# Out projection and down products of the samples' 64 tokens: two products instead of three

## The chip, the cores and the metric

The kernel runs on one core of a Trainium2 chip. The metric is the device time of one execution in microseconds (us), and the number compared is the median of several. Engines are named as in the profile: PE (TensorE, with PEld for its weight loads), DVE (VectorE), ACT (ScalarE), POOL (GpSimd) and SP (SyncE, which here only issues DMAs).

## The reference, cut to what matters

One layer of a hybrid decoder (sparse attention beside a gated delta rule) runs over 1024 prompt tokens and over 64 sample tokens (8 sequences of 8) with the same weights. The change touches its last part, which works on a token axis of 1088 rows:

```
mix = concat([o_a, o_b])              # 1088 x 1024, attention heads and delta rule heads
x   = x + mix @ w_out                 # out projection, 1024 x 1024
hm  = rmsnorm(x, norm_mlp)
x   = x + square(relu(hm @ w_up)) @ w_down     # up 1024 x 4096, down 4096 x 1024
y   = rmsnorm(x, norm_final)
```

All of it is float32.

## The kernel before

**Splitting.** TensorE multiplies in a rounded float32 form (fp32r). To keep precision, each operand is split: ScalarE rounds it (`hi`), and VectorE subtracts that from the original (`lo`). `split_product` (lines 2533 to 2535) then issues three products into one PSUM bank: hi x hi, hi x lo of the weights, lo of the activations x hi. The fourth, lo x lo, is left out.

**Sizes.** P is 128, D is 1024, KD = 8 is D in blocks of 128, TOK is 1088 tokens, SEQ is 1024, NS is 64. Tokens come in NT + 1 = 9 row blocks: t = 0 to 7 are 128 prompt tokens each, and t = 8 (t == NT) is the samples' 64. `rows_of(t)` gives 128 or 64. Output columns come in two halves (i = 0, 1) of 512, one PSUM bank each.

**Out projection** (`stage_output_projection`). Three groups g of three row blocks, six banks each (bank j holds row block 3g + j // 2, half j % 2). In each group the loop runs over the 8 blocks f of the contraction and over the six banks, three products each, with the activations as the stationary operand and 512 columns of the weights moving. The rounded weights come through a ring of three blocks: DMA on SP, cast on ACT (L2631), subtraction on DVE (L2668). The activations `mix` are rounded into `h_hi` (L2634) and `h_lo` (L2672). When a group's banks are complete, DVE adds all six to `x2` (L2710), and then, in the next group's loop, each row block is squared and rooted on ACT (L2641, L2643), scaled on DVE (L2677, L2681), transposed on PE (L2600), multiplied by the gain on DVE (L2692), and split again for the MLP (L2662 on ACT, L2696 on DVE). For the third group, which holds row blocks 6, 7 and 8, there is no next group, and this work stands alone at the end of the stage. DVE adds all six banks there before it scales row block 6.

**MLP** (`stage_mlp`). 32 blocks of 128 hidden columns. An "up" step makes one of them for all tokens (three pieces of 364, 364 and 360 tokens in banks 0 to 3, with the weights stationary). A "down" step takes two of them (e = 2f and 2f + 1) and runs over the nine row blocks and both halves: six products in one of the banks 4 to 7, in rotation, which DVE then adds to `x2` (L2908). The order is written out by hand in `steps`: up 0, up 1, then for each of 16 down steps "up 2g + 2, down g, up 2g + 3". PE waits for bank n of a down step until addition n - 4 is done. Behind a down step's additions DVE makes the low parts of the next two blocks of down weights (L2873, after ACT's cast L2830), and then the squares of the next up step (L2918, after ACT's relu L2847). The hidden activations are split by ACT (L2852) and DVE (L2888) into `hid_hi` and `hid_lo`. In the last down step (step 15) DVE also does the final norm: behind row block t's additions comes `final(t - 1)` (L2880, L2882), which waits for ACT's squares and root of that row block (L2860, L2863), and at the end `final(7)` and `final(8)`.

The samples' row block t = 8 is the last of each down step and of the third group. Its products are 64 columns of the stationary wide and leave the upper 64 partitions of their bank unused.

## Time and profile before

| | |
|---|---|
| median of the runs | 2143.38 us (3 runs, 2138.87 to 2144.5) |
| profiled execution | 2143.51 us |
| its span, first to last instruction | 2141.7 us |
| mean granted TensorE clock | 0.945 |
| PE busy | 1924.3 us, 90% of the span |
| DVE busy | 1178.0 us, 55% |
| ACT busy | 682.3 us, 32% |
| POOL busy | 251.6 us, 12% |

The out projection runs from about 1222 to 1346 us of the span (its first cast to its last DVE operation), and the MLP from there to the end. Matmuls are pipelined, so the recorded length of one is longer than the distance from its start to the next one's start. Where products follow each other, it is that distance that counts.

### The profile page before, as it was taken

To read this page: it belongs to the slowest core of one execution; us is meant where nothing else is said; L and a number is where in the kernel's file an instruction comes from. 1 tells how busy PE (TensorE), PEld (TensorE's weight loads), DVE (VectorE), ACT (ScalarE), POOL (GpSimd) and SP (SyncE) were. 2 spreads that over 40 slices of the span, in tenths; PEclk is the share of its full clock that TensorE was granted. 3 is DMA by queue.
4 is the path that set the end of the run, shared out by engine and by line. 5 is a ranking of instruction groups with operands and counts; after the bars stand their busy time and mean duration, and the time that the engine had idled before them with its cause. 6 is when DMAs were issued, how large, how long until landed. Compare 5 with 4: busy or idle time off the path is not lost. (4 is left out here: it accounts for less than half of the span.)

```text
span 2141.7 us, 33279 instructions
## 1 busy us (share of the span) xinstructions
PE 1924.3 (90%) x12648; PEld 1601.5 (75%) x12648; DVE 1178.0 (55%) x2298; ACT 682.3 (32%) x1373; POOL 251.6 (12%) x294
## 2 busy tenths in 40 slices
PE   5999999883589986898999699799999999999998
PEld 5888899883278874566544287788888999998886
DVE  3275588999556646764333266344444444444446
ACT  5332257652423322553322144321111212221113
POOL 4324332210211000001133100000000000000000
PEclk8999999996699996999999799899999999999999
DMA  5324322110110004404898452211111111111102
GB/s 147 80 66 128 87 80 60 30 40 0 51 41 2 2 2 158 143 1 140 291 325 299 145 197 65 69 62 48 40 40 40 40 40 50 40 42 67 40 30 84
DMA packets 121931, 177.33 MB, mean 83 GB/s; under 512 B 33208, under 2 KB 73785, under 8 KB 121644
## 3 DMA queue, kind: packets, MB, share of 16 engines
q1 hardware_dynamic: 104428, 118.05, 17.0%
q0 software_dynamic: 17344, 57.16, 8.5%
q8 instruction: 100, 1.64, 0.3%
q14 instruction: 59, 0.48, 0.1%
HBM read 156.64 MB, written 18.01 MB: 82 GB/s over the span
## 5 line engine op out<-in xcount | busy, mean ns | idle before, releaser
L2533 PE MATMUL banks<-front_h_hi,front_w_hi 128*128 128x364 f32 (+2 forms) x744 | 257.7, 346 | 23.8 <-POOL front_w_lo L627 9.9
L2533 PE MATMUL banks<-h_hi,ml_up_hi 128*128 128x364 f32 (+1 forms) x768 | 253.2, 330 | 10.1 <-DVE ml_up_lo L2869 10.1
L2534 PE MATMUL banks<-h_lo,ml_up_hi 128*128 128x364 f32 (+1 forms) x768 | 253.1, 329 | 0.0
L2535 PE MATMUL banks<-h_hi,ml_up_lo 128*128 128x364 f32 (+1 forms) x768 | 253.0, 329 | 0.0
L2534 PE MATMUL banks<-front_h_lo,front_w_hi 128*128 128x364 f32 (+2 forms) x744 | 250.0, 336 | 0.0
L2535 PE MATMUL banks<-front_h_hi,front_w_lo 128*128 128x364 f32 (+2 forms) x744 | 250.0, 336 | 0.0
L2908 DVE TENSOR_TENSOR x<-x,banks 128x512 f32<-128x512 f32 x256 | 175.8, 687 | 125.5 <-PE banks L2535 125.3
L2533 PE MATMUL banks<-ml_down_hi,ml_hid_hi 128*128 128x512 f32 (+1 forms) x576 | 224.5, 390 | 2.5 <-DVE ml_hid_lo L2888 2.5
L2534 PE MATMUL banks<-ml_down_lo,ml_hid_hi 128*128 128x512 f32 (+1 forms) x576 | 224.4, 390 | 0.0
L2535 PE MATMUL banks<-ml_down_hi,ml_hid_lo 128*128 128x512 f32 (+1 forms) x576 | 224.1, 389 | 0.0
L296 DVE TENSOR_SCALAR_CACHE_REDUCE work<-arena,work 128x384 bf16<-128x384 f32 (+5 forms) x194 | 176.1, 958 | 1.0 <-issue 0.3
L2533 PEld LDWEIGHTS banks<-front_h_hi,front_w_hi 128*128 128x128 f32 (+1 forms) x744 | 143.5, 193 | 41.5 <-POOL front_w_lo L627 11.8
L2918 DVE TENSOR_TENSOR arena<-arena 128x364 f32<-128x364 f32 (+1 forms) x96 | 51.6, 537 | 209.7 <-ACT arena L2847 209.7
L2533 PEld LDWEIGHTS banks<-h_hi,ml_up_hi 128*128 128x128 f32 x768 | 145.0, 189 | 11.7 <-DVE ml_up_lo L2869 10.3
L2534 PEld LDWEIGHTS banks<-h_lo,ml_up_hi 128*128 128x128 f32 x768 | 145.1, 189 | 0.7
L2535 PEld LDWEIGHTS banks<-h_hi,ml_up_lo 128*128 128x128 f32 x768 | 145.0, 189 | 0.0
L2534 PEld LDWEIGHTS banks<-front_h_lo,front_w_hi 128*128 128x128 f32 (+1 forms) x744 | 143.6, 193 | 0.8
L2535 PEld LDWEIGHTS banks<-front_h_hi,front_w_lo 128*128 128x128 f32 (+1 forms) x744 | 143.0, 192 | 0.9
L2830 ACT CAST ml_down_hi<-arena 128x1024 fp32r<-128x1024 f32 x32 | 32.1, 1048 | 293.9 <-PE banks L2535 293.5
L2533 PEld LDWEIGHTS banks<-ml_down_hi,ml_hid_hi 128*128 128x128 f32 (+1 forms) x576 | 104.7, 182 | 27.4 <-DVE ml_hid_lo L2888 2.8
L2535 PEld LDWEIGHTS banks<-ml_down_hi,ml_hid_lo 128*128 128x128 f32 (+1 forms) x576 | 104.7, 182 | 26.2
L2534 PEld LDWEIGHTS banks<-ml_down_lo,ml_hid_hi 128*128 128x128 f32 (+1 forms) x576 | 104.7, 182 | 25.3
(432 smaller groups left out, 3276.1 us busy)
## 6 DMA issues: line engine op xcount, KB each, us to landing
upper<-in_cache_k SPq DMA_DIRECT2D x128, 256.0 KB, 3.9
upper<-in_cache_v POOLq DMA_DIRECT2D x112, 256.0 KB, 4.3
arena<-in_w_up SPq DMA_DIRECT2D x32, 512.0 KB, 4.1
arena<-in_w_down SPq DMA_DIRECT2D x32, 512.0 KB, 5.5
work<-in_w_in POOLq DMA_DIRECT2D x30, 512.0 KB, 4.6
op_raw<-in_w_out SPq DMA_DIRECT2D x24, 512.0 KB, 3.7
arena<-in_x_prompt SPq DMA_DIRECT2D x8, 512.0 KB, 5.9
upper<-in_cache_v SPq DMA_DIRECT2D x16, 256.0 KB, 3.8
```

Of the source, the lines that this page charges most:

```text
L296: dve.tensor_scalar(junk, sc[0:rows, :], than, 0.0, op, ALU.add, accum_out=out[0:rows, i:i + 1]).then_inc(self.counted, 1)
L2533: pe.matmul(out, lh, rh, start=start, stop=False)
L2534: pe.matmul(out, lh, rl, start=False, stop=False)
L2535: return pe.matmul(out, ll, rh, start=False, stop=stop)
L2830: act.copy(dhi[:, n % 2, :], raw_down[:, n % 2, :]).then_inc(down_hi, 1)
L2908: dve.tensor_tensor(part, part, k.psum[4 + n % 4][0:r, :], ALU.add).then_inc(added, 1)
L2918: dve.tensor_tensor(tmp[:, j, 0:w], tmp[:, j, 0:w], tmp[:, j, 0:w], ALU.mult).then_inc(squared, 1)
```

## The change

For the samples' row block the high and the low part of the activations now lie side by side: `h_hi` gets 64 more columns (1088 to 1151), and the low part of the samples' 64 columns is written there instead of into `h_lo`; `hid_hi` likewise, while `hid_lo` loses its 64. One product with these 128 columns as the stationary gives hi x hi in the bank's partitions 0 to 63 and lo x hi in 64 to 127. A second product, with the 64 high columns, adds hi x (weights' lo) to partitions 0 to 63. That makes two products instead of three (`split_product_samples`). DVE then adds the upper half of the bank to `x2` and, after a wait for that (semaphore `low_added`), the lower half: two additions in place of one.

Each subtraction that makes a low part and covers the samples' columns becomes two instructions, since they go to different tensors.

```diff
--- before.py
+++ after.py
@@ -226,7 +226,7 @@
         x2 = enter(nc.sbuf_tensor("x2", [P, NT, D], F32))
         self.x2 = [x2[:, t, :] for t in range(NT)] + [self.view(self.hT_at, D)]
         self.x2_prompt = x2
-        self.h_hi = enter(nc.sbuf_tensor("h_hi", [P, KD, TOK], F32R))
+        self.h_hi = enter(nc.sbuf_tensor("h_hi", [P, KD, TOK + NS], F32R))
         self.h_lo = enter(nc.sbuf_tensor("h_lo", [P, KD, TOK], F32R))
 
     def sem(self, name):
@@ -2535,6 +2535,17 @@
     return pe.matmul(out, ll, rh, start=False, stop=stop)
 
 
+def split_product_samples(pe, bank, both, right, start, stop):
+
+
+    rh, rl = right
+    if start:
+        pe.matmul(bank, both, rh, start=True, stop=False)
+        return pe.matmul(bank[0:NS, :], both[:, 0:NS], rl, start=False, stop=False)
+    pe.matmul(bank[0:NS, :], both[:, 0:NS], rl, start=False, stop=False)
+    return pe.matmul(bank, both, rh, start=False, stop=stop)
+
+
 def stage_output_projection(k):
 
 
@@ -2560,6 +2571,7 @@
              "squared", "rooted", "rstd", "normed", "turned", "kept", "rounded", "rest")
     (mix_hi, mix_lo, w_hi, w_lo, made, used, added,
      squared, rooted, scaled, normed, turned, kept, rounded, rest) = (k.sem("op_" + n) for n in names)
+    low_added = k.low_added = k.sem("low_added")
     xp = a["x_prompt"][0].rearrange("(t p) d -> p t d", p=P)
     xs = a["x_sample"].rearrange("b t d -> (b t) d")
     wv = a["w_out"][0].rearrange("(k p) n -> p k n", p=P)
@@ -2614,7 +2626,10 @@
                             cols = slice(t * P, t * P + rows_of(t))
                             left = k.h_hi[:, f, cols], k.h_lo[:, f, cols]
                             right = whi[:, (g * KD + f) % RING, i * 512:(i + 1) * 512], wlo[:, (g * KD + f) % RING, i * 512:(i + 1) * 512]
-                            last = split_product(pe, k.psum[j][0:rows_of(t), :], left, right, f == 0, f == KD - 1)
+                            if t < NT:
+                                last = split_product(pe, k.psum[j], left, right, f == 0, f == KD - 1)
+                            else:
+                                last = split_product_samples(pe, k.psum[j], k.h_hi[:, f, SEQ:TOK + NS], right, f == 0, f == KD - 1)
                             if f == KD - 1:
                                 last.then_inc(made, 1)
                         if f < KD - 1:
@@ -2631,7 +2646,7 @@
                 act.copy(whi[:, n % RING, :], raw[:, n % RING, :]).then_inc(w_hi, 1)
 
             def round_mix(f):
-                act.copy(k.h_hi[:, f, :], mix[:, f, :]).then_inc(mix_hi, 1)
+                act.copy(k.h_hi[:, f, 0:TOK], mix[:, f, :]).then_inc(mix_hi, 1)
 
             def length(t):
                 r = rows_of(t)
@@ -2669,7 +2684,8 @@
 
             def rest_of_mix(f):
                 dve.wait_ge(mix_hi, f + 1)
-                dve.tensor_tensor(k.h_lo[:, f, :], mix[:, f, :], k.h_hi[:, f, :], ALU.subtract).then_inc(mix_lo, 1)
+                dve.tensor_tensor(k.h_hi[:, f, TOK:], mix[:, f, SEQ:], k.h_hi[:, f, SEQ:TOK], ALU.subtract)
+                dve.tensor_tensor(k.h_lo[:, f, 0:SEQ], mix[:, f, 0:SEQ], k.h_hi[:, f, 0:SEQ], ALU.subtract).then_inc(mix_lo, 1)
 
             def scale(t):
                 r = rows_of(t)
@@ -2707,6 +2723,9 @@
                         r = rows_of(t)
                         part = k.x2[t][0:r, i * 512:(i + 1) * 512]
                         dve.wait_ge(made, NP * (g - 1) + j + 1)
+                        if t == NT:
+                            dve.tensor_tensor(part, part, k.psum[j][NS:P, :], ALU.add).then_inc(low_added, 1)
+                            dve.wait_ge(low_added, i + 1)
                         dve.tensor_tensor(part, part, k.psum[j][0:r, :], ALU.add).then_inc(added, 1)
                     n = g * KD + f + RING - 1
                     if n < KD:
@@ -2730,6 +2749,7 @@
     up_sem, down_sem = k.sems("ml_up_landed", 2), k.sems("ml_down_landed", 2)
     names = ("up_rounded", "up_rest", "down_rounded", "down_rest", "up", "relu", "square", "hid_rounded", "hid_rest", "down", "added")
     up_hi, up_lo, down_hi, down_lo, upped, relued, squared, hid_hi, hid_lo, downed, added = (k.sem("ml_" + n) for n in names)
+    low_added, LOW_BEFORE = k.low_added, 2
     wu = a["w_up"][0].rearrange("(k p) n -> p k n", p=P)
     wd = a["w_down"][0].rearrange("(k p) n -> p k n", p=P)
 
@@ -2753,7 +2773,7 @@
         assert m.at <= LASTING
         uhi, ulo = sbuf("up_hi", [2, KD, P]), sbuf("up_lo", [2, KD, P])
         dhi, dlo = sbuf("down_hi", [2, D]), sbuf("down_lo", [2, D])
-        hhi, hlo = sbuf("hid_hi", [3, TOK]), sbuf("hid_lo", [3, TOK])
+        hhi, hlo = sbuf("hid_hi", [3, TOK + NS]), sbuf("hid_lo", [3, SEQ])
         block = ctx.enter_context(nc.Block())
 
         @block.sync
@@ -2811,8 +2831,12 @@
                             pe.wait_ge(added, n - 3)
                         for e in (2 * f, 2 * f + 1):
                             cols, half = slice(t * P, t * P + r), slice(i * 512, (i + 1) * 512)
-                            last = split_product(pe, k.psum[4 + n % 4][0:r, :], (hhi[:, e % 3, cols], hlo[:, e % 3, cols]),
-                                                 (dhi[:, e % 2, half], dlo[:, e % 2, half]), e == 2 * f, e == 2 * f + 1)
+                            right = dhi[:, e % 2, half], dlo[:, e % 2, half]
+                            if t < NT:
+                                last = split_product(pe, k.psum[4 + n % 4], (hhi[:, e % 3, cols], hlo[:, e % 3, cols]), right,
+                                                     e == 2 * f, e == 2 * f + 1)
+                            else:
+                                last = split_product_samples(pe, k.psum[4 + n % 4], hhi[:, e % 3, SEQ:TOK + NS], right, e == 2 * f, e == 2 * f + 1)
                         last.then_inc(downed, 1)
 
         @block.scalar
@@ -2885,7 +2909,10 @@
             def rest_hidden(f, j):
                 at, w = pieces[j]
                 dve.wait_ge(hid_hi, 3 * f + j + 1)
-                dve.tensor_tensor(hlo[:, f % 3, at:at + w], tmp[:, j, 0:w], hhi[:, f % 3, at:at + w], ALU.subtract).then_inc(hid_lo, 1)
+                prompt = min(at + w, SEQ) - at
+                if prompt < w:
+                    dve.tensor_tensor(hhi[:, f % 3, TOK:], tmp[:, j, prompt:w], hhi[:, f % 3, SEQ:TOK], ALU.subtract)
+                dve.tensor_tensor(hlo[:, f % 3, at:at + prompt], tmp[:, j, 0:prompt], hhi[:, f % 3, at:at + prompt], ALU.subtract).then_inc(hid_lo, 1)
 
             for f in range(2):
                 rest_up(f)
@@ -2905,6 +2932,9 @@
                         dve.wait_ge(downed, n + 1)
                         if f:
                             dve.wait_ge(added, n - ND + 1)
+                        if t == NT:
+                            dve.tensor_tensor(part, part, k.psum[4 + n % 4][NS:P, :], ALU.add).then_inc(low_added, 1)
+                            dve.wait_ge(low_added, LOW_BEFORE + 2 * f + i + 1)
                         dve.tensor_tensor(part, part, k.psum[4 + n % 4][0:r, :], ALU.add).then_inc(added, 1)
                         if f == F // 2 - 1 and i and t:
                             final(t - 1)
```

The places where instructions stand differently are these. TensorE, the last row block of the last down step, t = 8, before (`ml_down_hi` and `ml_down_lo` are the weights' parts, `ml_hid_hi` and `ml_hid_lo` the activations'; the shape is stationary columns x moving columns):

```order
L2534 MATMUL banks<-ml_down_lo,ml_hid_hi 128x512
L2535 MATMUL banks<-ml_down_hi,ml_hid_lo 128x512
L2533 MATMUL banks<-ml_down_hi,ml_hid_hi 64x512
L2534 MATMUL banks<-ml_down_lo,ml_hid_hi 64x512
L2535 MATMUL banks<-ml_down_hi,ml_hid_lo 64x512
```

The first two belong to t = 7. Three products of 64 columns stand for each hidden block, so a half (512 output columns) has six. The same place of the changed kernel:

```order
L2535 MATMUL banks<-ml_down_hi,ml_hid_lo 128x512
L2543 MATMUL banks<-ml_down_hi,ml_hid_hi 128x512
L2544 MATMUL banks<-ml_down_lo,ml_hid_hi 64x512
L2545 MATMUL banks<-ml_down_lo,ml_hid_hi 64x512
L2546 MATMUL banks<-ml_down_hi,ml_hid_hi 128x512
```

The first row is t = 7 again. Four products make a half, two for each hidden block. The second hidden block's products stand in reversed order (narrow, wide). TensorE has 80 instructions fewer over the program. VectorE, the end of the last down step, before (`x` is `x2`; `arena` on the left of an addition is the samples' row block of it):

```order
L2908 TENSOR_TENSOR x<-x,banks 128x512 x2
L2880 RECIPROCAL arena<-arena 128x1
L2882 SCALAR_TENSOR_TENSOR x<-x,arena 128x1024
L2908 TENSOR_TENSOR arena<-arena,banks 64x512 x2
L2880 RECIPROCAL arena<-arena 128x1
L2882 SCALAR_TENSOR_TENSOR x<-x,arena 128x1024
L2880 RECIPROCAL arena<-arena 64x1
```

The row with x2 is the samples' two additions. The same place of the changed kernel:

```order
L2938 TENSOR_TENSOR x<-x,banks 128x512 x2
L2904 RECIPROCAL arena<-arena 128x1
L2906 SCALAR_TENSOR_TENSOR x<-x,arena 128x1024
L2936 TENSOR_TENSOR arena<-arena,banks 64x512
L2938 TENSOR_TENSOR arena<-arena,banks 64x512
L2936 TENSOR_TENSOR arena<-arena,banks 64x512
L2938 TENSOR_TENSOR arena<-arena,banks 64x512
L2904 RECIPROCAL arena<-arena 128x1
```

There are four, and each of L2938 waits for the L2936 ahead of it. At the end of the projection VectorE has in the changed kernel:

```order
L2729 TENSOR_TENSOR x<-x,banks 128x512 x4
L2727 TENSOR_TENSOR arena<-arena,banks 64x512
L2729 TENSOR_TENSOR arena<-arena,banks 64x512
L2727 TENSOR_TENSOR arena<-arena,banks 64x512
L2729 TENSOR_TENSOR arena<-arena,banks 64x512
```

Before, the last four rows were one row of two additions; the scaling of row block 6 follows them in both.

## Rows read from the trace of the kernel before

**Rows 1.** The page's chain that ended last, shares by engine.

```profile
PE 36%; DMA 0%; DVE 0%; ACT 0%; issue 0%
```

**Rows 2.** Stretches: us, busy of PE, PEld, DVE, ACT, POOL; clock, DMA share, GB/s.

```profile
1275.00:1300.00 25.00, 25.00 (x120) 20.80 (x119) 16.30 (x23) 10.90 (x16) 0.00 (x0) 1.00 0.39 126
...
1504.00:1553.00 49.00, 49.00 (x256) 44.00 (x255) 23.35 (x35) 9.19 (x16) 0.00 (x0) 1.00 0.13 44
```

**Rows 3.** PE's timeline, the projection's end: start, us, engine, line, operation.

```profile
1336.19 1.09 PE L2600 MATMUL banks<-arena 128*128 128x128 f32 x8 [1.71 <-DVE arena L2681]
1338.76 1.94 PE L2600 MATMUL banks<-arena 128*128 128x128 f32 x8 [1.48 <-DVE arena L2692]
```

**Rows 4.** DVE's timeline, the projection's end.

```profile
1331.17 2.66 DVE L2710 TENSOR_TENSOR x<-x,banks 128x512 f32<-128x512 f32 x4 [2.22 <-PE banks L2535]
1333.83 1.38 DVE L2710 TENSOR_TENSOR arena<-arena,banks 64x512 f32<-64x512 f32 x2
1335.13 0.15 DVE L2677 RECIPROCAL arena<-arena 128x1 f32<-128x1 f32 x1
1335.38 0.76 DVE L2681 TENSOR_SCALAR arena<-x,arena 128x1024 f32<-128x1024 f32 x1
```

**Rows 5.** DVE's timeline, the end of the last down step.

```profile
2133.94 1.45 DVE L2908 TENSOR_TENSOR arena<-arena,banks 64x512 f32<-64x512 f32 x2
2135.31 0.15 DVE L2880 RECIPROCAL arena<-arena 128x1 f32<-128x1 f32 x1
2135.50 1.28 DVE L2882 SCALAR_TENSOR_TENSOR x<-x,arena 128x1024 f32<-128x1024 f32 x1
```

**Rows 6.** ACT's timeline, the samples' squares of the final norm.

```profile
2135.42 1.02 ACT L2860 ACTIVATE banks<-arena 64x1024 f32<-64x1024 f32 x1 [1.28 <-DVE arena L2908]
```

**Rows 7.** PE's timeline, down step 14: t = 8 and its neighbours.

```profile
2092.28 0.39 PE L2535 MATMUL banks<-ml_down_hi,ml_hid_lo 128*128 128x512 f32 x1
2092.50 0.40 PE L2533 MATMUL banks<-ml_down_hi,ml_hid_hi 128*64 128x512 f32 x1
2092.74 0.39 PE L2534 MATMUL banks<-ml_down_lo,ml_hid_hi 128*64 128x512 f32 x1
...
2095.03 0.39 PE L2535 MATMUL banks<-ml_down_hi,ml_hid_lo 128*64 128x512 f32 x1
2095.26 0.33 PE L2533 MATMUL banks<-h_hi,ml_up_hi 128*128 128x364 f32 x1
```

**Rows 8.** DVE's timeline, behind down step 14.

```profile
2095.46 0.68 DVE L2908 TENSOR_TENSOR arena<-arena,banks 64x512 f32<-64x512 f32 x1 [0.70 <-PE banks L2535]
2096.60 2.36 DVE L2873 TENSOR_TENSOR ml_down_lo<-arena,ml_down_hi 128x1024 fp32r<-128x1024 f32 x2 [0.46 <-ACT ml_down_hi L2830]
2099.96 0.54 DVE L2918 TENSOR_TENSOR arena<-arena 128x364 f32<-128x364 f32 x1 [1.00 <-ACT arena L2847]
...
2108.38 1.42 DVE L2888 TENSOR_TENSOR ml_hid_lo<-arena,ml_hid_hi 128x364 fp32r<-128x364 f32 x3
```

**Rows 9.** Waits from 1240 us on: who, for whom; us, times, longest.

```profile
DVE x L2908 <- PE banks L2535: 125.3, 230, 1.7
```

**Rows 10.** PE's timeline, the first product of down step 15.

```profile
2109.85 0.50 PE L2533 MATMUL banks<-ml_down_hi,ml_hid_hi 128*128 128x512 f32 x1 [2.47 <-DVE ml_hid_lo L2888]
```

**Rows 11.** Stretches as in rows 2, short ones, for the granted clock.

```profile
1219.60:1221.00 1.40, 0.63 (x4) 0.40 (x4) 0.64 (x4) 0.00 (x0) 0.00 (x0) 1.00 0.04 12
1221.00:1222.00 1.00, 0.00 (x0) 0.00 (x0) 0.75 (x5) 0.00 (x0) 0.00 (x0) 0.90 0.00 0
...
1337.80:1338.00 0.20, 0.00 (x0) 0.00 (x0) 0.20 (x2) 0.00 (x0) 0.00 (x0) 0.65 0.00 0
...
2109.00:2110.00 1.00, 0.15 (x1) 0.15 (x2) 0.80 (x2) 0.06 (x1) 0.00 (x0) 1.00 0.00 0
```

**Rows 12.** The chain in order of time (start, us, what): two down steps.

```profile
2044.19 0.23 PE banks L2533
...
2092.66 0.24 PE banks L2533
```

## The prediction

> **What bounds the kernel now.** I read the chain of waits first: its share is 36% TensorE and nothing else that rounds to a percent [rows 1]. It is followed back only to the start of the MLP stage, so it says that this stage is one unbroken TensorE stream, and little of what lies before. The table by stretches says the same and adds the output projection: in 25 us of the projection and in 49 us of the MLP, TensorE is busy for 25.00 and 49.00 us at a granted clock of 1.00, while VectorE is busy for 16.30 and 23.35 and ScalarE for 10.90 and 9.19 [rows 2]. So a TensorE instruction taken out of the stream there is worth its pitch (start to start) as long as the others keep up. Its recorded length of 0.39 us is not the price, since products overlap.
>
> The stream has two places where it is not the bound, and the samples' rows stand last in both: the end of the projection, where VectorE's additions, a norm and transposes follow one another with TensorE idle [rows 3, 4], and the last down step with the final norm [rows 5, 6].
>
> **Products taken out.** The samples' 64 rows (row block t = 8) now take 2 products of 512 columns for each weight row block and column half where they took 3. Down steps: 16 steps x 2 halves x 2 row blocks x 1 = 64 fewer. Projection: 8 x 2 x 1 = 16 fewer. The pitch is read in down step 14: the 12 products of 64 rows start at 2092.50 and the stream goes on at 2095.26, so 2.76 / 12 = 0.230 us each [rows 7]. Half the width does not make a product cheaper: the row before them, 128 wide, stands 0.22 before the next.
>
> Not all 80 count. In the last down step and in the last row block of the projection's third group, what follows t = 8 is VectorE, which is already occupied (below). So 15 x 4 = 60 down products and 7 x 2 = 14 projection products remain: 60 x 0.230 = 13.8 us and 14 x 0.230 = 3.2 us. **Gain 17.0 us.**
>
> The widened product has 128 stationary columns where it had 64. Its pitch is bounded by the rows at 2092.28 (0.22, 128 wide) and 2092.50 (0.24, 64 wide) [rows 7]; I take 0.230, and either end moves the sum by under 0.7 us.
>
> **Additions put in.** For t = 8 VectorE now adds the bank's lower half and then its upper half: 2 more additions of 64x512 in each down step and in the projection, 34 in all. An addition takes 0.68 us [rows 8]. The second of a pair waits for the first one's result. What such a wait costs has two rows: the operation after the reciprocal at 1335.13 (0.15 long) starts 0.10 after its end [rows 4], and that after the one at 2135.31 starts 0.04 after [rows 5]. So a pair takes 0.67 back to back plus 0.76, which is 1.43 us, and two pairs 2.86 us. The bounds are 4 x 0.65 = 2.6 (four additions took 2.66 [rows 4]) and 4 x 0.79 = 3.16.
>
> A row shows only additions that all start at the same partition. The Trainium skill, "VectorE: DVE Perf Modes", section "Two Vector instructions with no wait between them", says that an instruction whose input starts in another group of 32 partitions than the last one read from that memory is held until all earlier ones have finished. By it the first of each pair would wait too, and each tail below would be 0.2 us longer, which gives 2130.8 in place of 2130.4. No row here shows it.
>
> *In down steps 0 to 14* they are covered. VectorE waits about half a microsecond before an addition (125.3 us over 230 of them, 0.54 each [rows 9]). With the change the two halves of t = 8 are ready at about 2093.6 and 2094.5 (2092.50 + 4 and 8 x 0.23, and 0.2 for the last product to end), two pairs of additions end at 2093.6 + 2.9 = 2096.5, where the rest of the down weights began at 2096.60 because of ScalarE [rows 8]. They end at about 2098.8; the next squares, at 2099.96 before, come 0.92 earlier at 2099.0. So the cover that was 1.00 us of idle time [rows 8] shrinks to 0.2 us but holds. If it did not, squares would start late, and TensorE waits for those only through ScalarE's rounding a whole up step later. Cost 0. Queued behind the new wait on VectorE are just these rests.
>
> *At the projection's end* nothing covers them. The samples' additions start at 1333.83 behind four others and the reciprocal of row block 6 follows at 1335.13, 1.30 us later [rows 4]. The last four products shrink in time, but VectorE gets to t = 8 at 1333.83 anyway. Now 2.86 us pass: **+1.6 us**. Everything behind (norm, transposes, the weights' loading that begins with the next stage) moves with it.
>
> *In the last down step* VectorE has additions and final norms without a pause: the samples' two additions start at 2133.94 with no wait in their row, and ScalarE's squares follow at 2135.42, 1.48 later [rows 5, 6]. Now 2.86 + 0.02: **+1.4 us**, and TensorE's 0.92 us are not seen at all, since its last product no longer ends the wait.
>
> **Clock.** TensorE's first transposes at the projection's end start at 1336.19, 1.71 us idle behind the products, and 8 of them take 1.09 us. The next 8, at 1338.76, take 1.94 [rows 3]; the granted clock went from 1.00 to 0.50 (2.4 to 1.2 GHz) within 1337.80 to 1338.00 [rows 11]. With the change TensorE ends 0.46 earlier there and the transposes start 1.6 later, so it idles for 3.8 us. In one place the clock fell within 1221 to 1222, under 2 us after TensorE's last work; in another it stood at 1.00 after 2.5 us idle [rows 10, 11]. So the first eight transposes can run at the low clock: 1.94 - 1.09 = **+0.85 us**, or 0. I take 0.85, since 3.8 us is longer than both of these waits. A fall that comes earlier does not change what follows, which already runs at 0.50.
>
> **Smaller.** Each subtraction that makes the low part splits in two where the samples' columns are in it: one more VectorE instruction, between 0 and 0.15 us (the length of a one-column reciprocal [rows 4]). There are 8 in the projection, where VectorE has 8 us free in 25, and 32 in the MLP. The only exposed one is before down step 15, where TensorE waits 2.47 us for three of them in a row [rows 8, 10]: **+0.1 us**. ScalarE, the DMA queues and their order are untouched.
>
> **Sum.** -17.0 + 1.6 + 1.4 + 0.85 + 0.1 = -13.0 us. The profiled execution took 2143.5 us (its span 2141.7), the median of the runs shown is 2143.4, so nothing has to be shifted: **2130.4 us**, or 0.6% faster. A measurement of this kernel can tell about 0.3%, 6.4 us. With the bounds of the terms the sum lies between -14.5 and -12.0. The three runs lie from 2138.9 to 2144.5, which adds 3 us on either side: 2126 to 2134 for this case.
>
> **Rivals.**
> *Changes of width stall the array* (slower). After the change 128-column and 64-column stationaries alternate: 128, 64, 64, 128 for each half of a down step, 4 changes a step, 64 in all, and 4 in each of 8 blocks of the projection, 96 together against 48 before. If each emptied and restarted the array, the price would be that of a restart: the first product after a wait is recorded with 0.50 us [rows 10] against the pitch of 0.23, so 0.27. 96 x 0.27 = 25.9, less the 13.0 gained: +12.9, 2156 us. From 0.14 us a change on it loses. Against it: the changes that exist cost 0.01 to 0.02 (0.22 before and 0.24 after the step from 128 to 64, 0.23 from 64 to 128) [rows 7]. The Trainium skill, "TensorEngine Tiling (Array Packing)", section "Key Properties", says that changing the tiling mode drains TensorE; if a 64-column product is another mode here, the rule speaks for this rival, and the trace speaks against it. 5%.
>
> *VectorE's additions reach TensorE in the down steps.* With a cover of only 0.2 us, a slip of 0.5 us in each of 15 steps that reached TensorE would take 7.5 of the 13 us: 2138. Against it: TensorE had no wait at all in the steady steps (49.00 of 49.00 us [rows 2]), with four banks in rotation. 8%.
>
> *The tails cost less.* The clock stays up and the additions run back to back (2.6): the sum becomes -17.0 + 1.3 + 1.1 = -14.6, or, were the last steps' 6 products to count too, -16: 2127.5. 12%.
>
> The rest, 75%, is the forecast.
>
> **Numbers.** Range 2125 to 2136: it holds the forecast's 2126 to 2134, the cheap tails and the near side of the second rival. It leaves out the first rival and most of the second. Faster by over 0.3% (under 2137.0): 75 + 12 and, for a smaller slip in the second rival, 1, which is 88%. Within 0.3%: the rest of the second rival, 7%. Slower by over 0.3%: the first rival, 5%.
>
> **What would show it.** Right: a period of 47.55 us from down step to down step where it was 48.47 [rows 12], eight products at t = 8 with a pitch of 0.23, no new TensorE wait in the MLP. At the projection's end the samples' four additions take 2.9 us and the first transposes 1.9. After the last product, the end of the work comes 2.3 us later than before, 1.4 of it the additions and 0.9 the shorter stream. Wrong: a pitch above 0.24 at a change of width, a TensorE wait for additions, or a tail that grows by more than 2 us.

## The result

The changed kernel takes 2131.74 us (median of 7 executions, 2127.68 to 2133.13) against 2142.21 us of the kernel before on the same chip (7 executions, 2138.87 to 2148.27). The ratio is 0.9945, with a 95% interval from 0.9932 to 0.9957: 0.55% faster. The profiled execution took 2131.74 us, its span is 2130.0 us, against 2143.5 and 2141.7 before.

The page's busy times and the chain:

```profile
PE 1906.2 (89%) x12568; PEld 1595.3 (75%) x12568; DVE 1202.3 (56%) x2372; ACT 682.4 (32%) x1373; POOL 251.6 (12%) x294
...
PE 36%; DVE 0%; DMA 0%; ACT 0%; issue 0%
```

TensorE is 18.1 us less busy and VectorE 24.3 us more, the price of 34 added additions and 40 split subtractions. The other engines still round to 0% of the chain, as in [rows 1].

**The steady part** (PE's timeline in down step 14, the samples' eight products and what follows):

```profile
2078.48 0.39 PE L2543 MATMUL banks<-ml_down_hi,ml_hid_hi 128*128 128x512 f32 x1
2078.70 0.40 PE L2544 MATMUL banks<-ml_down_lo,ml_hid_hi 128*64 128x512 f32 x1
2078.94 0.39 PE L2545 MATMUL banks<-ml_down_lo,ml_hid_hi 128*64 128x512 f32 x1
2079.17 0.39 PE L2546 MATMUL banks<-ml_down_hi,ml_hid_hi 128*128 128x512 f32 x1
...
2080.31 0.33 PE L2533 MATMUL banks<-h_hi,ml_up_hi 128*128 128x364 f32 x1
```

Eight products start from 2078.48 on and the up step follows at 2080.31, so 1.83 us, 0.229 each, where twelve took 2.76 [rows 7]. The chain in order of time gives the period between down steps 13 and 14:

```profile
2031.32 0.23 PE banks L2544
...
2078.87 0.24 PE banks L2544
```

47.55 us where it was 48.47 [rows 12]: 0.92 us less a step, four products. VectorE's timeline behind the same step:

```profile
2079.59 0.69 DVE L2936 TENSOR_TENSOR arena<-arena,banks 64x512 f32<-64x512 f32 x1 [0.23 <-PE banks L2546]
...
2082.36 2.34 DVE L2897 TENSOR_TENSOR ml_down_lo<-arena,ml_down_hi 128x1024 fp32r<-128x1024 f32 x2
2085.01 0.54 DVE L2948 TENSOR_TENSOR arena<-arena 128x364 f32<-128x364 f32 x1 [0.31 <-ACT arena L2871]
```

The two pairs of additions take 2.77 us to the start of the weights' rests, and the squares still find VectorE 0.31 us idle, where it had been 1.00 [rows 8]. TensorE never waits for it: 49.00 of 49.00 us busy, as before [rows 2]:

```profile
1504.00:1553.00 49.00, 49.00 (x257) 44.44 (x256) 24.97 (x40) 9.19 (x16) 0.00 (x0) 1.00 0.13 44
```

**The projection's end** (DVE's and PE's timelines), against [rows 3, 4]:

```profile
1328.41 2.66 DVE L2729 TENSOR_TENSOR x<-x,banks 128x512 f32<-128x512 f32 x4 [1.77 <-PE banks L2535]
1331.10 0.69 DVE L2727 TENSOR_TENSOR arena<-arena,banks 64x512 f32<-64x512 f32 x1
1331.82 0.68 DVE L2729 TENSOR_TENSOR arena<-arena,banks 64x512 f32<-64x512 f32 x1
1332.54 0.69 DVE L2727 TENSOR_TENSOR arena<-arena,banks 64x512 f32<-64x512 f32 x1
1333.26 0.68 DVE L2729 TENSOR_TENSOR arena<-arena,banks 64x512 f32<-64x512 f32 x1
1333.87 0.15 DVE L2693 RECIPROCAL arena<-arena 128x1 f32<-128x1 f32 x1
```

```profile
1330.88 0.40 PE L2546 MATMUL banks<-op_w_hi,h_hi 128*128 128x512 f32 x1
1334.93 1.97 PE L2612 MATMUL banks<-arena 128*128 128x128 f32 x8 [3.66 <-DVE arena L2697]
```

From the samples' first addition to the reciprocal of row block 6 it is now 2.77 us (1.30 before). TensorE is idle for 3.66 us (1.71 before), and its first eight transposes take 1.97 us (1.09 before), at the low clock.

**The last down step** (PE, DVE and ACT), against [rows 5, 6, 10]:

```profile
2094.97 0.60 PE L2533 MATMUL banks<-ml_down_hi,ml_hid_hi 128*128 128x512 f32 x1 [2.54 <-DVE ml_hid_lo L2915]
2095.37 0.63 PE L2534 MATMUL banks<-ml_down_lo,ml_hid_hi 128*128 128x512 f32 x1
...
2120.07 0.39 PE L2546 MATMUL banks<-ml_down_hi,ml_hid_hi 128*128 128x512 f32 x1
```

```profile
2120.78 0.69 DVE L2936 TENSOR_TENSOR arena<-arena,banks 64x512 f32<-64x512 f32 x1
...
2122.94 0.68 DVE L2938 TENSOR_TENSOR arena<-arena,banks 64x512 f32<-64x512 f32 x1
```

```profile
2123.66 1.02 ACT L2884 ACTIVATE banks<-arena 64x1024 f32<-64x1024 f32 x1 [2.79 <-DVE arena L2938]
```

From the first of the samples' additions to ScalarE's squares it is now 2.88 us, against 1.48. From the start of TensorE's last product (2120.07) to the end of the span it is 9.93 us, against 7.43 before (from 2134.27), so 2.50 more where 2.3 was forecast. And here is something that the kernel before did not show in its profile: after the wait of 2.54 us TensorE's products stand 0.43 us apart, not 0.23, until 2098.7. The granted clock in stretches, with the columns of [rows 2]:

```profile
2094.60:2095.00 0.40, 0.03 (x1) 0.03 (x1) 0.31 (x1) 0.00 (x0) 0.00 (x0) 1.00 0.00 0
2095.00:2095.40 0.40, 0.40 (x2) 0.29 (x3) 0.00 (x0) 0.00 (x0) 0.00 (x0) 0.78 0.00 0
2095.40:2095.80 0.40, 0.40 (x3) 0.30 (x2) 0.00 (x0) 0.00 (x0) 0.00 (x0) 0.50 0.00 0
...
2098.60:2099.00 0.40, 0.40 (x3) 0.32 (x3) 0.00 (x0) 0.00 (x0) 0.00 (x0) 0.96 0.00 0
```

In this profile it fell to 0.50 at about 2095.2, 0.25 us after TensorE had begun again, and stood there for 3.4 us.

**Where the time went.** These are distances between rows of the timelines, in us: (a) from the first product of the projection to the samples' first addition at its end, (b) from there to the end of the stage's last VectorE operation, (c) to the first product of the MLP, (d) to the first product of the last down step, (e) to the samples' first addition there, (f) to ScalarE's squares of the samples, (g) to the end of the span.

| kernel | start | a | b | c | d | e | f | g | span |
|---|---|---|---|---|---|---|---|---|---|
| before | 1228.03 | 105.80 | 12.20 | 8.15 | 755.67 | 24.09 | 1.48 | 6.28 | 2141.7 |
| changed | 1227.56 | 103.54 | 14.55 | 6.92 | 742.40 | 25.81 | 2.88 | 6.34 | 2130.0 |
| difference | -0.5 | -2.3 | +2.3 | -1.2 | -13.3 | +1.7 | +1.4 | +0.1 | -11.7 |

### The profile page after: what moved, and what is told of

It is laid out like the page before. It is cut to its first block and busy times, and to the rows that moved or that the text cites. A ratio compares the mean times of both kernels' runs of the same rounds, so it can differ in the third digit from the quotient of the medians.

```text
span 2130.0 us, 33193 instructions
## 1 busy us (share of the span) xinstructions
PE 1906.2 (89%) x12568; PEld 1595.3 (75%) x12568; DVE 1202.3 (56%) x2372; ACT 682.4 (32%) x1373; POOL 251.6 (12%) x294
## 5 line engine op out<-in xcount | busy, mean ns | idle before, releaser
L2533 PE MATMUL banks<-front_h_hi,front_w_hi 128*128 128x364 f32 (+2 forms) x744 | 256.4, 345 | 25.2 <-POOL front_w_lo L627 10.1
L2938 DVE TENSOR_TENSOR x<-x,banks 128x512 f32<-128x512 f32 x256 | 175.7, 686 | 126.2 <-PE banks L2535 126.0
L2533 PE MATMUL banks<-ml_down_hi,ml_hid_hi 128*128 128x512 f32 x512 | 200.0, 391 | 2.5 <-DVE ml_hid_lo L2915 2.5
L2534 PE MATMUL banks<-ml_down_lo,ml_hid_hi 128*128 128x512 f32 x512 | 200.0, 391 | 0.0
L2535 PE MATMUL banks<-ml_down_hi,ml_hid_lo 128*128 128x512 f32 x512 | 199.8, 390 | 0.0
L2871 ACT ACTIVATE arena<-banks 128x364 f32<-128x364 f32 (+1 forms) x96 | 45.5, 474 | 240.1 <-PE banks L2535 240.1
L2533 PEld LDWEIGHTS banks<-ml_down_hi,ml_hid_hi 128*128 128x128 f32 x512 | 96.6, 189 | 22.4 <-DVE ml_hid_lo L2915 2.8
L2535 PEld LDWEIGHTS banks<-ml_down_hi,ml_hid_lo 128*128 128x128 f32 x512 | 96.6, 189 | 20.2
```

Of the source, the lines that this page charges most:

```text
L2533: pe.matmul(out, lh, rh, start=start, stop=False)
L2534: pe.matmul(out, lh, rl, start=False, stop=False)
L2535: return pe.matmul(out, ll, rh, start=False, stop=stop)
L2871: act.activation(tmp[:, j, 0:w], k.psum[n % 4][:, 0:w], ACT.Relu).then_inc(relued, 1)
L2938: dve.tensor_tensor(part, part, k.psum[4 + n % 4][0:r, :], ALU.add).then_inc(added, 1)
```

## The experiments

The theory is that of the prediction: a removed product is worth its pitch where TensorE's stream goes on, the added additions cost something at the two tails alone, and the clock adds its part there. Its rivals are that changes of width cost, that the additions reach TensorE in the steady steps, and that the projection gains in proportion to its products. The changed kernel's profile raised one more question: whether the low clock in the last down step is the change's doing.

All are compared with the kernel before, run in between on the same chip: e1 to e4 share one chip, e5 to e8 another, e9 to e11 a third. The medians of the kernel before were 2142.21 us beside the changed kernel's first executions, then 2142.15, 2142.35 and 2142.66. The ratio is an estimate from all executions, so it can differ from the quotient of two medians (for e8 that is 0.9913). Medians in us:

| run | median | executions | ratio to before | 95% interval |
|---|---|---|---|---|
| changed kernel | 2131.74 | 7 | 0.9945 | 0.9932 to 0.9957 |
| e1_down_only | 2131.78 | 6 | 0.9959 | 0.9943 to 0.9975 |
| e2_proj_only | 2144.15 | 11 | 1.001 | 1.000 to 1.002 |
| e3_wide_low | 2132.25 | 4 | 0.9959 | 0.9944 to 0.9975 |
| e4_no_low_in_steps | 2126.98 | 4 | 0.9938 | 0.9919 to 0.9957 |
| e5_no_low_in_tails | 2127.02 | 5 | 0.9936 | 0.9913 to 0.9958 |
| e6_samples_added_late | 2130.54 | 6 | 0.9948 | 0.9929 to 0.9967 |
| e7_early_last_step | 2127.72 | 5 | 0.9930 | 0.9905 to 0.9955 |
| e8_both | 2123.80 | 6 | 0.9927 | 0.9903 to 0.9950 |
| e9_change_again | 2131.06 | 5 | 0.9945 | 0.9927 to 0.9964 |
| e10_both_again | 2125.63 | 6 | 0.9915 | 0.9895 to 0.9935 |
| e11_down_early | 2128.13 | 5 | 0.9932 | 0.9914 to 0.9950 |

The intervals are some 0.2 to 0.5% wide, so most of these runs are told apart by their profiles, with the distances of the table above:

| run | a | b | c | d | e | f |
|---|---|---|---|---|---|---|
| e1_down_only | 106.49 | 12.20 | 8.04 | 741.66 | 24.21 | 2.87 |
| e2_proj_only | 103.55 | 14.55 | 6.85 | 756.34 | 25.71 | 1.49 |
| e3_wide_low | 102.92 | 14.55 | 6.67 | 742.48 | 25.82 | 2.88 |
| e4_no_low_in_steps | 102.24 | 13.84 | 6.72 | 742.01 | 25.72 | 2.88 |
| e5_no_low_in_tails | 103.47 | 12.28 | 6.81 | 741.95 | 25.59 | 1.30 |
| e6_samples_added_late | 105.99 | 11.45 | 6.75 | 742.67 | 25.81 | 2.88 |
| e7_early_last_step | 103.45 | 14.53 | 6.83 | 739.69 | 24.11 | 2.88 |
| e8_both | 105.83 | 11.46 | 7.21 | 739.56 | 24.12 | 2.88 |
| e9_change_again | 103.53 | 14.55 | 6.75 | 742.41 | 25.83 | 2.88 |
| e10_both_again | 105.68 | 11.46 | 6.76 | 738.71 | 24.11 | 2.88 |
| e11_down_early | 109.01 | 12.20 | 6.70 | 739.80 | 24.11 | 2.88 |

### One part of the change at a time

e1 puts the projection back to three products, one addition and one subtraction:

```diff
-                            if t < NT:
-                                last = split_product(pe, k.psum[j], left, right, f == 0, f == KD - 1)
-                            else:
-                                last = split_product_samples(pe, k.psum[j], k.h_hi[:, f, SEQ:TOK + NS], right, f == 0, f == KD - 1)
+                            last = split_product(pe, k.psum[j][0:rows_of(t), :], left, right, f == 0, f == KD - 1)
...
-                        if t == NT:
-                            dve.tensor_tensor(part, part, k.psum[j][NS:P, :], ALU.add).then_inc(low_added, 1)
-                            dve.wait_ge(low_added, i + 1)
```

> Only the down steps are changed; the projection is as before. Theory A (each product taken out of an unbroken stream is worth 0.23 us, the added additions are hidden in down steps 0 to 14 and bare in the last one): -13.8 + 1.4 + 0.1 = -12.3 us against before, ratio 0.994; down step period 47.55 us. Theory B (the added additions reach TensorE in the steady steps): the period is above 47.8 us and there are TensorE waits in the MLP. Either: the granted clock just after the wait ahead of the last down step can be high or low from one execution to the next, 1.7 us apart.

Measured: 0.9959, a median 10.4 us below the one of before, with the expected -12.3 us (0.9943) at the edge of the interval; the period is 47.55 us. All of the change's difference in d is there (741.66 against 742.40), and f is 2.87.

e2 is the reverse: the down steps as before, the projection changed.

> Only the projection is changed; the down steps are as before, with a period of 48.47 us. Theory A: 14 products gain 3.2 us, two more additions at the stage's end cost 1.5, and the first eight transposes at the low clock 0.9, so -0.8 us: no difference that can be measured, ratio 1.000. From the samples' first addition to the end of the stage 14.5 us (before: 12.2). Rival (the whole change's gain is proportional to the 16 of 80 products): -2.4 us or more.

Measured: 1.001, 1.000 to 1.002, a median 2.0 us above the one of before. A fifth of the removed products (16 of 80) gives no gain that the medians show. Its b is 14.55, the same as the changed kernel's to the hundredth, and takes back the 2.3 us of a. The rival, a gain in proportion, is out. In this profile TensorE waited 9.0 us for blocks of weights in the projection, where the profile of before has 8.1 (from the lists of waits). Without these waits a and b together are 109.1 us against 109.9, which is the 0.8 us that was expected. Why the median still lies above the one of before is taken up below, with the clock.

### Does a change of width cost?

```diff
         pe.matmul(bank, both, rh, start=True, stop=False)
-        return pe.matmul(bank[0:NS, :], both[:, 0:NS], rl, start=False, stop=False)
-    pe.matmul(bank[0:NS, :], both[:, 0:NS], rl, start=False, stop=False)
+        return pe.matmul(bank, both, rl, start=False, stop=False)
+    pe.matmul(bank, both, rl, start=False, stop=False)
```

> As the changed kernel, but the second product of a pair is also 128 stationary columns wide (it then also multiplies the low parts of both, a term the others leave out), so no product changes the width any more. Theory A (the width and its changes cost nothing): same as the changed kernel within 0.5 us by the period, 47.55 us, pitch 0.227 to 0.230 us at the samples' products. Rival (changes of width cost): the period falls by 4 times the price of a change; by 0.3 us or more if the price is worth naming.

Measured: its chain in order of time, at the same product of down steps 13 and 14:

```profile
2031.47 0.23 PE banks L2544
...
2079.00 0.23 PE banks L2544
```

47.53 us against 47.55. Its eight products (PE's timeline, 2078.61 to 2080.20 from the first start to the last) stand 0.227 apart.

So four changes of width a step cost 0.02 us together, at most 0.03, if a product of 128 stationary columns costs what one of 64 does; should one of them be dearer, this run shows only the sum of the two effects. The first rival of the prediction is out either way.

### The additions in the steady steps and in the tails

e4 leaves out the upper half's additions in down steps 0 to 14, so that part of the samples' sum is missing:

```diff
-                        if t == NT:
+                        if t == NT and f == F // 2 - 1:
                             dve.tensor_tensor(part, part, k.psum[4 + n % 4][NS:P, :], ALU.add).then_inc(low_added, 1)
-                            dve.wait_ge(low_added, LOW_BEFORE + 2 * f + i + 1)
+                            dve.wait_ge(low_added, LOW_BEFORE + i + 1)
```

e5 leaves out those in the projection and in the last down step:

```diff
                         dve.wait_ge(made, NP * (g - 1) + j + 1)
-                        if t == NT:
-                            dve.tensor_tensor(part, part, k.psum[j][NS:P, :], ALU.add).then_inc(low_added, 1)
-                            dve.wait_ge(low_added, i + 1)
...
-                        if t == NT:
+                        if t == NT and f < F // 2 - 1:
                             dve.tensor_tensor(part, part, k.psum[4 + n % 4][NS:P, :], ALU.add).then_inc(low_added, 1)
```

> As the changed kernel, but the additions of the bank's upper half are left out in down steps 0 to 14 (that part of the samples' sum is missing). Theory A (those 30 additions are fully covered): period 47.55 us as in the changed kernel, time the same within 0.3%. Theory B (they reach TensorE): up to 30 x 0.72 = 21.6 us faster, and any fall of the period below 47.5 us speaks for it.

Measured: the period is unchanged (chain in order of time):

```profile
2028.21 0.24 PE banks L2544
...
2075.76 0.23 PE banks L2544
```

47.55 us, and VectorE's idle time ahead of the squares is back at the 1.00 us of [rows 8] (its timeline):

```profile
2081.90 0.54 DVE L2948 TENSOR_TENSOR arena<-arena 128x364 f32<-128x364 f32 x1 [1.00 <-ACT arena L2871]
```

The 30 additions cost nothing in the steps. The theory by which they reach TensorE is out. Its median of four executions is 4.8 us lower than the changed kernel's. Its profile's span is 3.2 us shorter than that of the changed kernel. The MLP up to the last down step (d) accounts for 0.4 us of this; a, b, c and the stages ahead, where this kernel's instructions are the same, make up nearly all the rest. I take it as chance, and four executions cannot say more.

> As the changed kernel, but the additions of the bank's upper half are left out in the projection and in the last down step (that part of the samples' sum is missing). Theory A (these four are bare): 2 x 1.44 = 2.9 us less than the changed kernel, of which 1.44 between the samples' first addition and the reciprocal at the projection's end (2.77 becomes 1.3) and 1.44 between the samples' first addition and ScalarE's squares at the end (2.88 becomes 1.44); with the clock still high at the transposes another 0.9. Theory B (TensorE ends the tails too): no change there.

Measured: 0.9936, 2127.02 us. The four additions are bare, as expected and slightly more so: the distance from the samples' first addition to the reciprocal is 1.20 us (DVE's timeline) against 2.77 with them, and f is 1.30 against 2.88. So 1.57 and 1.58 us, against 1.44 expected. The two additions that are left also stand closer, 0.60 us apart where the four stand 0.72. These lines are from the projection's end:

```profile
1328.76 1.27 DVE L2726 TENSOR_TENSOR arena<-arena,banks 64x512 f32<-64x512 f32 x2
1329.96 0.15 DVE L2693 RECIPROCAL arena<-arena 128x1 f32<-128x1 f32 x1
```

```profile
1331.02 1.28 PE L2612 MATMUL banks<-arena 128*128 128x128 f32 x8 [1.97 <-DVE arena L2697]
```

The transposes took 1.28 us, between the 1.09 of the high and the 1.97 of the low clock, after a wait of 1.97 us. That the four additions delay both tails is shown; the theory by which TensorE ends the tails is out.

### Two rearrangements of the tails

e6 lets VectorE scale row blocks 6 and 7 first and adds the samples' sums behind them:

```diff
                     for j in range(NP if g and f == 0 else 0):
                         t, i = GT * (g - 1) + j // 2, j % 2
+                        if t == NT:
+                            continue
...
                         scale(GT * (g - 1) + scale_at[f])
+                    if g == NG and f == 1:
+                        add_samples()
```

> As the changed kernel, but at the projection's end VectorE scales row blocks 6 and 7 before it adds the samples' four sums, so that the transposes run beside the additions. Theory A: the transposes start about 1 us after TensorE's last product instead of 3.7 and take 1.1 us instead of 1.97; VectorE is then busy nearly without a pause, and the stage's end comes 1.5 to 2.0 us earlier relative to the samples' last product. If the additions were not what delays the transposes: no change.

Measured: 2130.54 us, 0.9948, no difference from the changed kernel that the medians show. In the profile the transposes start early and run at the high clock, as expected, but the stage ends only 0.5 us earlier: from TensorE's last product of the projection to the end it is 14.26 us (1335.28 to 1349.54) against 14.77 (1330.88 to 1345.65). The expected 1.5 to 2.0 us were wrong. PE's and DVE's timelines show why:

```profile
1336.74 1.09 PE L2612 MATMUL banks<-arena 128*128 128x128 f32 x8 [1.06 <-DVE arena L2705]
1342.27 1.94 PE L2612 MATMUL banks<-arena 128*128 128x128 f32 x8 [4.44 <-DVE arena L2716]
```

```profile
1335.66 0.16 DVE L2701 RECIPROCAL arena<-arena 128x1 f32<-128x1 f32 x1 [0.18 <-ACT arena L2658]
...
1337.03 0.16 DVE L2701 RECIPROCAL arena<-arena 128x1 f32<-128x1 f32 x1 [0.34 <-ACT arena L2658]
...
1340.85 1.27 DVE L2716 TENSOR_TENSOR arena<-banks,arena 128x512 f32<-128x512 f32 x2
```

The first transposes now wait 1.06 us instead of 3.66, but what they make is multiplied only at 1340.85, behind the additions, and the second eight wait 4.44 us for that. VectorE itself bounds this tail. The rearrangement could only fill VectorE's idle time ahead of the multiplication (1.13 us in the changed kernel), and it opened two waits for ScalarE's roots (0.18 and 0.34 us) that the additions had covered.

e7 removes the wait ahead of the last down step. In the last up step each piece is rounded and split as soon as it is squared, and the down step's row blocks wait for the piece that they need:

```diff
-                pe.wait_ge(hid_lo, 6 * (f + 1))
+                if f < F // 2 - 1:
+                    pe.wait_ge(hid_lo, 6 * (f + 1))
...
+                    if f == F // 2 - 1 and t in (0, 2, 5):
+                        pe.wait_ge(hid_lo, 3 * (F - 1) + {0: 1, 2: 2, 5: 3}[t])
...
                     act.activation(tmp[:, j, 0:w], k.psum[n % 4][:, 0:w], ACT.Relu).then_inc(relued, 1)
+                    if f == F - 1:
+                        act.wait_ge(downed, ND * ((f - 3) // 2 + 1))
+                        act.wait_ge(squared, n + 1)
+                        act.copy(hhi[:, f % 3, at:at + w], tmp[:, j, 0:w]).then_inc(hid_hi, 1)
...
+                    if f == F - 1:
+                        rest_hidden(f, j)
...
```

> As the changed kernel, but in the last up step each piece of hidden columns is rounded and split as soon as it is squared, and the last down step starts its first row blocks on the first piece. Theory A (2.5 us of TensorE wait and, where the clock falls in it, another 1.7 us are on the path through to the end): the wait ahead of the last down step falls from 2.5 us to under 0.5, the granted clock stays at 1.00 there, and the time from the last up step's last product to the end of the work falls by 2 to 2.5 us against the kernel before, 4 us against the changed kernel's profile. Rival (VectorE's final norms bound the last step anyway): the wait goes and the end does not move.

Measured: PE's timeline at the seam between the last up and the last down step:

```profile
2093.55 0.33 PE L2535 MATMUL banks<-h_hi,ml_up_lo 128*128 128x360 f32 x1
2093.72 0.39 PE L2533 MATMUL banks<-ml_down_hi,ml_hid_hi 128*128 128x512 f32 x1
2093.95 0.40 PE L2534 MATMUL banks<-ml_down_lo,ml_hid_hi 128*128 128x512 f32 x1
```

No wait, and the pitch is 0.23 from the start. d falls by 2.7 us and e by 1.7, to 24.11; together 4.4, about the 4 us that were expected against the changed kernel's profile. The rival fails: although VectorE has hardly a pause in the last down step, the whole step starts earlier. The times agree (0.9930), though the interval does not part it from the changed kernel by itself.

> As the changed kernel with both rearrangements of the two runs before it. Theory A: their gains add, 4 to 6 us below the changed kernel (0.2 to 0.3%), 0.75 to 0.85% below the kernel before. Rival: one of them only moves the wait, and it is not faster than the changed kernel.

Measured: 2123.80 us, 0.9927, which is 0.73% below the kernel before where 0.75 to 0.85 was expected. The changed kernel did not run on this chip, and the interval (0.9903 to 0.9950) holds both the forecast and the changed kernel's ratio.

> The changed kernel once more, on one chip with the next two, as the base for them. Theory A: 0.9945 of the kernel before within its interval; in the profile a period of 47.55 us; from the samples' first addition to the projection's end 13.8 or 14.55 us (clock high or low at the transposes), and from the first product of the last down step to the samples' first addition there 24.2 or 25.8 us, by the granted clock.

Measured: 2131.06 us, 0.9945, the ratio of the first time.

> Both rearrangements once more (samples added behind the scaling; last down step started on its first piece). From the profiles so far: the second one takes 2.7 us of wait from the MLP and keeps the clock high in the last down step (0 or 1.7 us), the first one only 0.5 us. So 3.2 to 4.9 us below the changed kernel of the same call, 0.15 to 0.23%. Rival: the lower medians so far came from the stages ahead of the projection, and the two agree within 0.1%.

Measured: 2125.63 us, 0.9915. That is 5.4 us below the changed kernel on the same chip, somewhat more than the 3.2 to 4.9 expected; the two intervals overlap by 0.0008. d is 3.7 and e 1.7 us shorter than in e9.

> Only the down steps changed, the projection as before, and the last down step started on its first piece. The projection's part of the change is worth about 0.8 us by the forecast and nothing by the run that had it alone. So this lies within 2 us of the run with both rearrangements, and 3 us or more below the changed kernel.

Measured: 2128.13 us, 0.9932, 2.5 us above e10 and 2.9 below e9, both just outside what was expected and well inside the intervals. In its profile d and e are those of e7, and the projection (a and b together) takes 121.2 us where e10 has 117.1. TensorE's waits for a block of weights in the projection make up 1.6 us of these 4.1 (10.1 against 8.5 us in all, from the lists of waits):

```profile
PE banks L2533 <- DVE op_w_lo L2680: 10.1, 2, 8.0
```

```profile
PE banks L2533 <- DVE op_w_lo L2683: 8.5, 2, 7.8
```

Another 1.7 us is the clock. The second of these waits lasted 2.08 us in e11, and behind it the stretches show the granted clock at 0.50 for 3.4 us:

```profile
1244.00:1246.00 2.00, 2.00 (x7) 1.54 (x6) 2.00 (x2) 2.00 (x3) 0.00 (x0) 0.50 0.70 246
1246.00:1248.00 2.00, 2.00 (x8) 1.59 (x7) 2.00 (x3) 0.40 (x1) 0.00 (x0) 0.68 0.81 223
```

In e10 the same wait lasted 0.75 us and the clock stayed at 1.00. That leaves about 0.8 us for the changed projection and its rearrangement.

The kernel with both rearrangements (e8 and e10) has the lowest medians of the study, 0.7 to 0.85% below the kernel before. Between the profiles of e9 and e10 lie 5.9 us. The early start of the last step gives 4.4 of them; 0.9 lie in a and b together, and 1.0 in a part of d that e7 and e8 do not show.

## Why the prediction was right, and where not

The forecast was 2130.4 us and a gain of 13.0 us; the medians gave 2131.74 and 10.5 us, the two profiles 11.8. So the time was met to 1.3 us and the gain came out 2.5 us smaller. By its steps:

**The pitch of a product, 0.230 us, and 60 down products: right.** 15 steps x 0.92 = 13.8 us, and the period shows 0.92. In d only 13.3 are seen, because TensorE's products ran at the low clock longer at the start of the MLP. There the slow ones stand 0.30 us apart and the fast ones 0.17 (PE's timeline of the changed kernel):

```profile
1352.57 0.67 PE L2533 MATMUL banks<-h_hi,ml_up_hi 128*128 128x364 f32 x1 [8.83 <-DVE ml_up_lo L2893]
...
1357.58 0.50 PE L2534 MATMUL banks<-h_lo,ml_up_hi 128*128 128x364 f32 x1
1357.88 0.36 PE L2535 MATMUL banks<-h_hi,ml_up_lo 128*128 128x364 f32 x1
1358.09 0.33 PE L2533 MATMUL banks<-h_hi,ml_up_hi 128*128 128x364 f32 x1
```

The clock was low from the first product at 1352.57 to about 1357.9, where the kernel before had 1354.18 to about 1358.3: 1.2 us more at half speed, so 0.6 us.

**14 projection products, 3.2 us: right, but 0.9 of it is not seen in a.** TensorE waited 9.2 instead of 8.1 us for weights in this stage. e1 and e11, with the old projection, show 8.8 and 10.1, and e3 and e4, with the new one, 8.7 and 7.8, so nothing ties this to the change.

```profile
PE banks L2533 <- DVE op_w_lo L2683: 9.2, 2, 7.9
```

**The covered additions: right.** The cover was put at 0.2 us and measured 0.31; e4 shows that taking the additions away leaves the period at 47.55 us.

**The two bare tails: right.** +1.6 was forecast at the projection's end and +1.47 measured (2.77 for 1.30); +1.4 in the last step and +1.40 measured. e5 gave 1.57 and 1.58 us for the same additions, because the kernel before had a little of this time as a wait for TensorE. Its last product (PE's timeline) ends at 2134.67, and the two additions that start at 2133.94 take 1.45 us [rows 5] where e5's, which wait for nothing, take 1.27:

```profile
2134.27 0.40 PE L2535 MATMUL banks<-ml_down_hi,ml_hid_lo 128*64 128x512 f32 x1
```

A pair takes 1.44 us, as the 1.43 of the forecast, but in two equal steps of 0.72 and not in 0.67 and 0.76. The second addition of a pair starts 0.03 us after the first one's end, below the lower of the two rows that bounded this wait. Here the Trainium skill's rule in "VectorE: DVE Perf Modes" ("Two Vector instructions with no wait between them") is seen at work. The addition at 1332.54 reads the bank from partition 64 where the one before read from 0, its products had been done for more than 0.8 us, and it starts 0.04 us after its predecessor's end, 0.72 after its start. Two additions that start at the same partition stand 0.60 us apart (e5 above). By the same rule the second of a pair would be held even without its wait, so these rows cannot part the price of the wait from that of the rule. The rule and the lower price of a wait nearly cancelled in the sum.

**The transposes at the low clock, +0.85: right in this profile (+0.88), and by chance in part.** Six profiles have this wait of 3.66 to 3.68 us. In five of them (this one, e2, e3, e7, e9) the transposes took 1.97 us, in e4 1.26. In e5, with 1.97 us of idle time ahead of them, they took 1.28, in e6 and e10, with 1.06 us, 1.09.

**The splitting of subtractions, +0.1: right.** The wait ahead of the last down step went from 2.47 to 2.54 us.

**What was missing: the clock in the last down step, +1.7 us.** The prediction took the 2.5 us wait there as one that leaves the clock alone, from the one profile it had, and even used it as the upper bound for waits that do no harm. In the nine profiles of this study that have this wait, the clock fell at it in seven. e2 shows that the fall does not need the changed down steps: it has those of the kernel before, its wait is 2.47 us, and yet (PE's timeline):

```profile
2109.41 0.63 PE L2533 MATMUL banks<-ml_down_hi,ml_hid_hi 128*128 128x512 f32 x1 [2.47 <-DVE ml_hid_lo L2912]
2109.84 0.63 PE L2534 MATMUL banks<-ml_down_lo,ml_hid_hi 128*128 128x512 f32 x1
```

The profile of before and that of e1 are the two that were spared. So a comparison of the changed kernel's profile with the profile of before charges the change with 1.7 us that the old down steps can have too. That they have them as often is not shown: of the two profiles with the old down steps one has the fall (e2), of the seven with the new ones six.

Every execution also has its mean granted clock on record, and here the two kernels differ. The kernel before had 0.944 to 0.954 in its 43 executions on the three chips of the experiments (median 0.949). The changed kernel had 0.942 to 0.947 in 12 executions (median 0.9445); on the chip that both share it is 0.944 in the mean against 0.948. In the kernel before the low clock goes with the long times: 11 executions at 0.946 or less have a median of 2143.6 us, 12 at 0.951 or more one of 2138.7. The profile of before, at 0.945, is one of the low ones. e2 fits in: 0.946 against 0.949 in its medians, and 2.0 us longer. So a part of what is missing from the forecast gain is probably time that the kernel before spends at the high clock and the changed one does not. The transposes at the projection's end are one such place. No kept profile shows the kernel before at its usual clock, so where the others are stays open, and so does their share.

**The rest** between the two profiles is stages that the change does not touch: the first weights of the MLP landed 1.2 us sooner (c; 8.2 and 8.0 us in the profiles of before and of e1, 6.7 to 7.2 in the other eleven), and the projection began 0.5 us sooner. With the missing terms the sum closes: -13.0 + 1.7 + 0.6 + 0.9 - 1.2 - 0.5 = -11.5, against -11.7 measured.

**The rivals.** Changes of width: out by e3 (0.02 us for the four changes of a step). The prediction charged this rival with all 96 changes, though 48 of them are in the time of before already. Only the 48 new ones count, so at 0.27 us each the rival gives 48 x 0.27 - 13.0 = 0, no loss and no gain, and not 2156 us; a loss begins at 0.27 us a change and not at 0.14. Additions that reach TensorE: out by e4. Cheaper tails: not what happened.

## What to carry to other kernels

An instruction taken out of an unbroken TensorE stream is worth its start-to-start pitch, times the number of places where the stream goes on. The last repetition of a loop, and the last group ahead of a serial tail, have to be counted apart: here the projection's 14 products saved their 3.2 us, and the tail behind them, where VectorE got the extra additions, took back 2.3.

When work is moved from the bounding engine to another one, look where that other one is last, and then whether it is itself full there. A reordering only fills idle time (e6: 0.5 us, where 1.5 to 2.0 were expected); starting the whole tail earlier moves all of it (e7: 2.7 us and the clock).

A single profile shows one outcome of a wait that sometimes costs the clock. Before such a wait is called harmless, look at the same place in another execution, or price it with a chance.

## What the runs showed of the hardware

- Stationaries of 128 and 64 columns alternate here from product to product at no price that counts: 0.229 us a product with the change of width, 0.227 without (512 moving columns, fp32r, granted clock 1.00). The Trainium skill's "TensorEngine Tiling (Array Packing)", "Key Properties", has a drain at each change of the tiling mode; the trace shows none for this pair.
- A wait of about 2.5 us on TensorE was followed by a granted clock of 0.50 (1.2 GHz) in seven of nine profiles. In five of them the fall came after TensorE had begun again, 0.2 to 1.0 us after the first product (here at 2095.2 us, with products from 2094.97 on; in e3 at 2096.1, with products from 2095.08 on). In e4 and e5 it came about 0.2 us before (the row below, for e4, whose first product starts at 2091.86). It cost 1.4 to 1.7 us (e against the 24.1 to 24.2 of the other profiles). Where the wait was removed (e7, e8, e10, e11) the clock stayed at 1.00 there in all four profiles. In e11 a wait of 2.08 us elsewhere was followed by the same fall.

```profile
2091.60:2091.80 0.20, 0.00 (x0) 0.00 (x0) 0.20 (x1) 0.00 (x0) 0.00 (x0) 0.68 0.00 0
```

- Additions on VectorE of 64x512 that read PSUM from partition 0 and from 64 in turn stand 0.72 us apart; those that stay at partition 0, 0.60 (e5).
